# A two-block network in one kernel on one core: the Ada modulation sums spread over both feed-forward parts, and 512-column passes in the gate, up and MLP projections

## The reference

```
def swiglu(x, w_gate, w_up, w_down):                       # both layers of the first network, width 2816
    return (jax.nn.silu(x @ w_gate) * (x @ w_up)) @ w_down

def squared_relu_mlp(h, w_in, w_out):                      # the second network, width 4096
    return jnp.square(jax.nn.relu(h @ w_in)) @ w_out
...
mod = jnp.split(jax.nn.silu(c) @ ada_w + ada_b, 6, axis=-1)   # c: 1 x 1024, ada_w: 1024 x 6144
a = modulate(rmsnorm(x, g_pre), mod[0], mod[1])               # h * (1 + scale) + shift
x = x + mod[2] * rmsnorm(short_gated_conv(a, ...), g_post)
x = x + mod[5] * rmsnorm(squared_relu_mlp(modulate(rmsnorm(x, g_pre_ff), mod[3], mod[4]), ...), g_post_ff)
```

## Time and profile before

| | before |
|---|---|
| median of 3 runs | 978.26 us (978.03 to 978.44) |
| the profiled execution, time | 977.55 us |
| its span, first to last instruction | 975.7 us |
| mean granted TensorE clock | 0.998 of 2.4 GHz |
| PE busy | 945.5 us (97%) |
| DVE busy | 646.3 us (66%) |
| ACT busy | 466.6 us (48%) |
| HBM | 190.5 MB, 194 GB/s over the span |

### The profile page before, as it was taken

One profiled execution on the slowest core, in us unless ns is written; L12 is line 12 of the kernel. 1 busy time (PEld: TensorE's weight loads), 2 busy tenths in 40 slices (PEclk: granted clock), 3 DMA queues, 4 the chain that ended last, 5 costly groups with the idle time before them and its releaser, 6 DMA issues.

```text
span 975.7 us, 15125 instructions
## 1 busy us (share of the span) xinstructions
PE 945.5 (97%) x6537; PEld 864.5 (89%) x6537; DVE 646.3 (66%) x737; ACT 466.6 (48%) x577; POOL 60.8 (6%) x79
## 2 busy tenths in 40 slices
PE   6999999999999999899899999999899999999997
PEld 6999889999999899776699989998899889999986
DVE  4966896545354873676659778789766865555554
ACT  6546844434343465755544343445354544444442
POOL 2024000000000000220030000000000000000000
PEclk9999999999999999999999999999999999999999
DMA  8743385655555454312579999995565456565531
GB/s 262 239 151 130 111 273 184 206 177 177 199 186 173 131 173 114 130 44 87 187 281 326 393 313 335 313 345 175 182 199 188 132 177 210 176 203 183 175 127 44
DMA packets 122282, 190.52 MB, mean 195 GB/s; under 512 B 6566, under 2 KB 103080, under 8 KB 119144
## 3 DMA queue, kind: packets, MB, share of 16 engines
q1 hardware_dynamic: 115184, 156.94, 49.5%
q0 software_dynamic: 5616, 31.78, 9.0%
q10 hardware_dynamic: 1416, 0.83, 0.3%
HBM read 188.49 MB, written 1.05 MB: 194 GB/s over the span
## 4 chain that ended last, share of the span: by engine, by line
PE 70%; DVE 9%; ACT 3%; issue 2%; DMA 1%; DVEq 0%; POOL 0%
PE PS L567 13%; PE PS L565 13%; PE PS L566 13%; PE PS L572 9%; PE PS L574 9%; PE PS L573 9%; DVE lo L1576 2%; ACT hi L1137 1%; PE PS L701 1%; DVE stats L1653 1%; PE PS L665 1%; DVE r L1646 1%; ACT hid L1438 1%; DVE x_tok L1666 1%; DVE gate_s L2007 1%
## 5 line engine op out<-in xcount | busy, mean ns | idle before, releaser
L1576 DVE TENSOR_TENSOR lo<-raw,hi 128x2048 fp32r<-128x2048 f32 (+2 forms) x150 | 336.4, 2258 | 167.3 <-ACT hi L1137 167.1
L565 PE MATMUL PS<-x_hi,hi 128*128 128x256 f32 x1320 | 375.2, 284 | 1.5 <-DVE x_lo L1773 1.5
L567 PE MATMUL PS<-x_hi,lo 128*128 128x256 f32 x1320 | 373.0, 283 | 0.0
L566 PE MATMUL PS<-x_lo,hi 128*128 128x256 f32 x1320 | 372.5, 282 | 0.0
L1137 ACT ACTIVATE hi<-raw 128x2048 fp32r<-128x2048 f32 (+2 forms) x150 | 278.1, 1880 | 10.5 <-DMA raw<-even_w_in 6.6
L565 PEld LDWEIGHTS PS<-x_hi,hi 128*128 128x128 f32 x1320 | 252.1, 191 | 3.9 <-DVE lo L1576 1.9
L566 PEld LDWEIGHTS PS<-x_lo,hi 128*128 128x128 f32 x1320 | 252.1, 191 | 1.9 <-issue 0.5
L567 PEld LDWEIGHTS PS<-x_hi,lo 128*128 128x128 f32 x1320 | 252.0, 191 | 0.0
L572 PE MATMUL PS<-hi,hid_hi 128*128 128x512 f32 x352 | 141.2, 401 | 0.7 <-DVE hid_lo L1847 0.5
L574 PE MATMUL PS<-hi,hid_lo 128*128 128x512 f32 x352 | 138.6, 394 | 0.0
L573 PE MATMUL PS<-lo,hid_hi 128*128 128x512 f32 x352 | 138.5, 394 | 0.0
(11 more groups left out here) (280 smaller groups left out, 824.9 us busy)
## 6 DMA issues: line engine op xcount, KB each, us to landing
raw<-ffn_w_gate SPq DMA_DIRECT2D x22, 1024.0 KB, 5.4
raw<-ffn_w_up SPq DMA_DIRECT2D x22, 1024.0 KB, 5.6
raw<-ffn_w_down SPq DMA_DIRECT2D x22, 1024.0 KB, 5.0
raw<-mlp_w_in SPq DMA_DIRECT2D x16, 1024.0 KB, 5.6
raw<-mlp_w_out SPq DMA_DIRECT2D x16, 1024.0 KB, 4.9
sq<-ada_w POOLq DMA_DIRECT2D x12, 1024.0 KB, 6.3
r<-ada_w POOLq DMA_DIRECT2D x12, 1024.0 KB, 7.0
raw<-sc_w_in SPq DMA_DIRECT2D x12, 1024.0 KB, 5.2
```

The source lines that it names most:

```text
L565: pe.matmul(dst, wh, hi, start=start, stop=False, skip_group_check=True)
L566: pe.matmul(dst, wh, lo, start=False, stop=False, skip_group_check=True)
L567: return pe.matmul(dst, wl, hi, start=False, stop=stop_, skip_group_check=True)
L1576: dve.tensor_tensor(split_view("lo", c), split_view("raw", c), split_view("hi", c).bitcast(F32), ALU.subtract)\
```

## The change

**Passes.** `x_hi` and `x_lo` become the two halves of one tensor `x_both`. The new helper `wide_cols` takes the place of `col` in the 53 chunks: the high weights meet both halves in one pass of 512 columns, then the low weights meet `x_hi` in a pass of 256. The second 256 columns of the bank (hi*lo) are a partial sum of their own, so each of the chunk's two column tiles needs a whole bank, gate takes banks 4 and 5, up takes 6 and 7 in every block, and the halves are added afterwards: ACT copies the low half out of PSUM, DVE adds the other half (`gate_s`, then `hid`), ACT applies silu, DVE multiplies. In the MLP the relu moves from ACT into DVE's squaring, behind such an addition.

**Ada.** 16 steps go to blocks 1 to 7 of `ffn0`, 8 to blocks 1 to 6 of `ffn1`. `modrow` is split into two fp32r parts in a new `mod_part` (ACT `mod_high`, DVE `mod_low`), and `mod_sums` makes four fp32r passes of 512 columns into banks 6 and 7. These stand behind the block's down projection in blocks 5, 6 and 8 of `ffn0` and 8 of `ffn1`; in block 10 of both parts they stand between the two halves of the tail. The first four rows are stored in HBM during the odd mixer, whose tiles lie on `modrow`, and are loaded back in `ffn1`. `mod_part` lies on the place of `lnrow`, so `ln1` and `ln3` load their gain and bias only after the part's last row sum. The rule that a block with three steps does one of them first is gone.

```
+            def wide_cols(c, bank, between=None):
+                pe.wait_ge(lo_split, c + 1)
+                for m in range(2):
...
+                    cols = slice(m * P, (m + 1) * P)
+                    for k in range(KT):
+                        wh, wl = slot("hi", c)[:, k, cols], slot("lo", c)[:, k, cols]
+                        pe.matmul(PS[:, bank + m, :], wh, x_both[:, :, k, :], start=k == 0, stop=False, skip_group_check=True)
+                        last = pe.matmul(PS[:, bank + m, 0:S], wl, x_hi[:, k, :], start=False, stop=k == KT - 1,
+                                         skip_group_check=True)
...
-        ADA_BLOCKS = range(1, 10)
-        MOD_AT = {4: 0, 5: 1, 7: 2, 8: 3, 10: 4}
-        MOD_LAST = 5
+        ADA_STEPS = {"ffn0": (0, 2 * KT), "ffn1": (2 * KT, ADA_N)}
+        ADA_BLOCKS = {"ffn0": 7, "ffn1": 6}
+        MOD_AT = {"ffn0": {5: 0, 6: 1, 8: 2, 10: 3}, "ffn1": {8: 4, 10: 5}}
...
             pool.wait_ge(*sig_at("ln0", "x", 4))
+            ada_loads(0, 4)
+            pool.wait_ge(sem("mod_sum"), 4)
             ln_rows("ln1")
...
                 for n in range(2):
-                    last = pe.matmul(PS[:, bank + n, :], ones[:, :], modrow[:, m, n * HB:(n + 1) * HB], start=True, stop=True)
+                    for part in range(2):
+                        last = pe.matmul(PS[:, bank + n, :], ones_r[:, :], mod_part[:, part, n * HB:(n + 1) * HB],
+                                         start=part == 0, stop=part == 1, skip_group_check=True)
...
+                    wide_cols(at[name, "g", i] + 1, 6)
                     if i <= NF - TAIL:
                         pe.wait_ge(hid_lo_ok, ob + i)
                         rows_full(*down(i - 1), i == 1)
+                        if i in MOD_AT[name]:
+                            pe.wait_ge(hid_done, o + i + 2)
+                            mod_sums(MOD_AT[name][i], 6)
                 for h in range(2):
+                    if h:
+                        pe.wait_ge(hid_done, o + NF + 1)
+                        mod_sums(MOD_AT[name][NF - 1], 6)
...
-                    if ada and i == 1:
-                        dve.wait_ge(sem("silu_c_ready"), 1)
-                        dve.wait_ge(sem("ada_bias"), 16)
...
-                    if len(ada) > 2:
-                        ada_step(dve, ada.pop(0))
...
-                        split(g + 3)
+                        split(g + 3 + (i == NF - 1))
+                        n = (NF - 1) * (name == "ffn1") + i
+                        dve.wait_ge(sem("low_part"), 2 * n - 1)
+                        dve.tensor_tensor(gate_s[:, i % 2, :, :], PS[:, 4:6, 0:S], gate_s[:, i % 2, :, :], ALU.add)\
+                           .then_inc(sem("gate_sum"), 1)
+                        dve.wait_ge(sem("low_part"), 2 * n)
+                        link(dve.tensor_tensor(hid[:, i % 2, :, :], PS[:, 6:8, 0:S], b_sb[:, i % 2, :, :], ALU.add))
                         dve.wait_ge(silu, o + i + 2)
-                        dve.wait_ge(chunk_used, g + 2)
-                        dve.tensor_tensor(hid[:, i % 2, :, :], gate_s[:, i % 2, :, :], bank2(7 - 2 * (i % 2)), ALU.mult)\
+                        dve.tensor_tensor(hid[:, i % 2, :, :], gate_s[:, i % 2, :, :], hid[:, i % 2, :, :], ALU.mult)\
                            .then_inc(hid_done, 1)
```

More of the change, by code:

```diff
@@ L554, in _ @@
             gain_row(1)
+            pool.wait_ge(sem("mod_sum"), 6)
+            ln_rows("ln3")
             pool.wait_ge(*sig_at("ln3", "x", 4))
@@ L594, in col @@
                                    hi[:, k, :], lo[:, k, :], k == 0, k == kt - 1)
+                last.then_inc(chunk_used, 1)
+            def wide_cols(c, bank, between=None):
+                pe.wait_ge(lo_split, c + 1)
+                for m in range(2):
+                    if between and m:
+                        between()
+                    cols = slice(m * P, (m + 1) * P)
[4 more added lines that the diff above has]
+                                         skip_group_check=True)
                 last.then_inc(chunk_used, 1)
@@ L718, in ffn @@
                 for i in range(1, NF):
-                    b = 6 - 2 * (i % 2)
-                    pe.wait_ge(hid_done, o + i)
-                    if name == "ffn1" and i - 1 in MOD_AT:
-                        pe.wait_ge(sem("mod_row"), MOD_AT[i - 1] + 1)
-                    col(at[name, "g", i], b, x_hi, x_lo)
+                    if i == 1:
+                        pe.wait_ge(hid_done, o + 1)
+                    else:
+                        pe.wait_ge(sem("ffn_silu"), o + i + 1)
+                    wide_cols(at[name, "g", i], 4)
                     if i == 1:
@@ L1213, in layer_norm, with mod_high @@
                 turned_hi(name, 1)
+            def mod_high(m):
+                act.wait_ge(sem("ada_fma"), KT * (m // 2 + 1))
+                if m:
+                    act.wait_ge(sem("mod_sum"), m)
+                act.activation(mod_part[:, 0, :], modrow[:, m, :], ACT.Copy).then_inc(sem("mod_high"), 1)
             def mod_copy(m, bank):
@@ L1244, in ffn @@
                     act.activation(hid_hi[:, i % 3, :, :], hid[:, i % 2, :, :], ACT.Copy).then_inc(hi_done, 1)
-                    if name == "ffn1" and i in MOD_AT:
-                        mod_copy(MOD_AT[i], 6 - 2 * ((i - 1) % 2))
-                    if i < NF - 1:
-                        split(g + 4)
+                    if i in MOD_AT[name]:
+                        mod_high(MOD_AT[name][i])
+                    split(g + 4 if i < NF - 1 else at[name, "d", i] + 2)
+                    if i in MOD_AT[name]:
+                        mod_copy(MOD_AT[name][i], 6)
             act.dma_start(const[:, 0:P], A["consts"][:, 0:P]).then_inc(sem("ident_landed"), 16)
@@ L1725, in gained, with mod_low @@
                                          op0=ALU.add, op1=ALU.mult).then_inc(sem("gained"), 1)
+            def mod_low(m):
+                dve.wait_ge(sem("mod_high"), m + 1)
+                dve.tensor_tensor(mod_part[:, 1, :], modrow[:, m, :], mod_part[:, 0, :].bitcast(F32), ALU.subtract)\
+                   .then_inc(sem("mod_low"), 1)
             def ffn(name):
@@ L1732, in ffn @@
                     g = at[name, "g", i]
[L1733 to L1736 removed]
+                    n0, n1 = ADA_STEPS[name]
+                    nb = ADA_BLOCKS[name]
+                    ada = list(range(n0 + (n1 - n0) * (i - 1) // nb, n0 + (n1 - n0) * i // nb)) if 1 <= i <= nb else []
+                    if i == 1:
+                        dve.wait_ge(sem("a_silu_c"), 2)
+                        dve.wait_ge(sem("ada_bias"), 16 + 16 * (name == "ffn1"))
                     split(g + 2)
[L1738 to L1739 removed]
                     if i == 0:
```

127 lines of the change are left out of this document (78 added, 49 removed).

## The result

| | before | after |
|---|---|---|
| median (17 runs each, same chip) | 978.33 us | 981.31 us (979.07 to 984.01) |
| ratio, 95% interval | | 1.0029 (1.0021 to 1.0038) |
| span of the profiled execution | 975.7 us | 978.9 us |
| mean granted TensorE clock | 0.998 | 0.993 |
| PE busy | 945.5 us | 939.3 us |

The change makes the kernel 0.3% slower, where I had forecast 0.1% faster. PE has less to do and the span is longer, so PE waits more. The page of the kernel after first: busy time, and the chain that ended last.

The account below looks back on a forecast made before the run. The prediction took PE, busy for 97%, to bound the kernel. Its terms, -5.9 - 4.9 + 5.5 + 2.6 + 1.7, summed to -1.0 us, for a median of 977.3 us, range 971 to 984.

Parts of the forecast that it names:

- wide passes: In 848 groups, one pass of 512 and one of 256 columns replace three of 256: 5.9 us less.
- row sums: Each row sum becomes four passes of 0.93 us instead of 1.72 us, four in PE's way: net 4.9 us less.
- waits for the low part: PE waits for mod_low in ffn0's blocks 5, 6 and 8, 2.3, 0.8 and 2.4 us: 5.5 us more.
- clock behind block 5's pause: In ffn0, a clock fall behind this pause was left out of the sum and named only in the clock rival.
- end of `ffn0`: Gain and bias load after the fourth row sum, so the norm ln1 slips by 2.6 us, bounds 1.3 to 4.
- end of `ffn1`: The bias lands at 15.9 us after the last up columns, needed at 14.2: the norm slips by 1.7 us.
- the +2.8 of the sum: Forecast sum if passes save only 2.1 us, by the Trainium skill's fixed 2.5 ns per pass, instead of 5.9.
- The clock rival: Slower, 20%: clock falls in new pauses at ffn0's end and around blocks 5 and 8, +3.9 us, giving 981.2 us.
- Work of DVE and ACT at nothing: Per block, ACT's two added copies and DVE's two additions cost nothing except where a row sum waits for them.

Follow-up runs that it names:

- e6: Changed kernel with gain and bias of ln1 and ln3 loaded early and the row sums' parts made early in ffn0's blocks 5, 6, 8: 970.19 us, ratio 0.9911.
- e8: e6 with each 512-column pass made as two of 256 columns: 976.11 us, ratio 0.998.
- e11: The changed kernel itself, run again for a second profile: 980.19 us, ratio 1.0022.
- e12: The changed kernel itself, run again for a third profile: 981.83 us.
- e1: Changed kernel with ffn0's row-sum parts laid on two unused rows of modrow, so ln1's gain and bias load early: 977.56 us, ratio 0.9995.
- e2: Changed kernel with ffn1's two row sums behind blocks 7 and 8, so ln3's gain and bias load early: 977.41 us, ratio 0.9996.
- e9: Kernel before, with only the gain and bias loads of ln1 and ln3 made late, after the tail's first half: 985.84 us, ratio 1.0079.
- e7: e6 with DVE's two products with the norm gains put back into ffn1's last block: 969.50 us, ratio 0.9904.
- e4: Changed kernel with each 512-column pass made as two of 256 columns: 984.15 us, ratio 1.0068.

## Why the prediction was wrong

| term | predicted | measured |
|---|---|---|
| wide passes | -5.9 | -6.3 (e6 against e8; the tails give back 0.4 of it) |
| row sums | -4.9 | -4.6 (1.01, 1.00, 1.02, 0.94 for four) |
| waits for the low part | +5.5 | +3.8 (2.05, 0.95, 0.8) |
| clock behind block 5's pause | 0 | +1.6 in the profiled execution, seldom otherwise |
| end of `ffn0` | +2.6 | +4.7: 3.3 the late norm, 1.4 the clock (+5.4 and +5.3 in e11 and e12) |
| end of `ffn1` | +1.7 | +3.9 |
| sum | -1.0 | +3.1; the span rose by 3.2 |

**Wide passes, row sums: right.** The 2.1 us that the Trainium skill's fixed cost per pass would give (TensorE: Matmul & The Clock Gate, on the back-to-back issue gap) do not hold here; e6 against e8 has three times that. That the +2.8 of the sum with them lies near the +3.1 measured is luck: the tails make up for it. My bounds for the saving, 3.6 and 7.1 us, don't follow from the rates that I gave: 848 x (0.238 - 0.2329) is 4.3 and 848 x (0.238 - 0.2288) is 7.8. The measured 6.3 lies inside either pair.

**Waits for the low part: right in kind, too large.** Block 5 came out nearly as worked out, 2.05 us for 2.3. For block 8 I had the second buffer's piece land after 7.0 us; DVE started on it 5.25 us after its issue, and PE waited 0.8 and not 2.4. The size hangs on a landing that differs between executions: block 5's pause was 1.9, 3.6 and 1.7 us in three profiles of the same program.

**The steps that failed: "End of *ffn0*" and "End of *ffn1*".** The mechanism was the one named, as e1, e2 and e9 show, and the terms were mis-sized, 4.3 together for 8.6. In `ffn0` the issue and the landing were 0.1 and 0.5 us later than worked out, so that the gain step slipped 3.3 us and not 2.6; the rest is the clock, which I had priced at nothing in the forecast. In `ffn1` the gain step came 18.0 us after U where I had 15.9: PE's wait for `hid_lo` was 1.3 us instead of 0.4 and put the row sum's end 1.1 later, POOL issued the bias 1.0 behind that and not 0.7, and it took 6.1 us to land instead of 5.3. e7 shows that the wait for `hid_lo` comes from the two products with the norm gains, as I had it, and is larger.

**The clock rival** had 20% and gave 981.2, almost the time measured. That is luck too: it had three falls for 3.9 us, and the 4.3 that the tails cost beyond my terms are not in it. Its place at the end of `ffn0` was right, with 1.4 us for my 1.3 (2.4 and 2.6 in e11 and e12). It was wrong for blocks 5 and 8 as a rule. Its condition, a pause and its turns as long as before 688, is no sharp limit: e2 met it at the end of `ffn0` with a pause of 3.57 us and kept the full clock, and block 5 of the first profile lost it behind 1.89. I had the evidence for the one place in my own text, a pause of 2.9 us and eight turns at the end of `ffn0`; it should have been in the sum there, and the rival for the others alone.

**Work of DVE and ACT at nothing: right inside the blocks.** e6 has no PE wait in any block from 1 to 10. It was wrong in `ffn0`'s tail: e1 and e6 still lose 1.1 to 1.3 us there against before, because the additions and the low part put the norm's start from +10.1 to +11.2 and +11.4. In the changed kernel this hid under the late bias.

## What to carry to other kernels

When a buffer is laid on another's place, work out when the load that now has to wait can be issued, with the engine's wake-up and the landing under that stretch's traffic, and who needs it first. A tensor that is idle in that stretch was there for the taking (two rows of `modrow`), and with it and two moved steps the same change is 0.9% faster instead of 0.3% slower. Price a long pause of TensorE (here 3.2 us and more) with the low clock behind it, here 1.3 to 2.7 us, not as the pause alone; and look at what else PE does around a short one, since at the end of `ffn1` two short pauses with eight turns between them were enough. And where PE waits for another engine further on, a saving on PE ahead of the wait can be partly given back (by the profiles 1.4 us of waits in e4, 0.4 in e8), so test it in a kernel that has the wait removed.
